# Two layers of a 16-expert MoE block: gate and up with the tokens stationary in layer 0, expert outputs added into SBUF in layer 1

## The reference, cut to what matters

```
aff = softmax(x @ w_router)               # (tokens, 16)
for segment in (latent: C = 64, context: C = 32):     # layer 1: latent only
    idx, g = the C tokens of the segment with the largest aff, for each expert
    xe = x[idx]                                        # (16, C, 1024)
    h  = silu(xe @ w_e_gate) * (xe @ w_e_up)           # (16, C, 1408)
    ye = (h @ w_e_down) * g
    out.at[idx].add(ye)                                # sum over the experts
```

## Time and profile before

| | us |
|---|---|
| median of 3 runs | 3777.25 (3774.8 to 3778.98) |
| the profiled execution: its own time | 3779.97 |
| its span | 3778.2 |
| PE busy | 3457.1 (92%) |
| DVE, ACT, POOL busy | 1099.1, 711.7, 130.8 |
| HBM read and written | 712.57 MB, 25.21 MB |

### The profile page before, as it was taken

The page is one execution under the profiler, slowest core; times in us unless marked ns, Lnnn a source line. Parts: engine busy times, 40 slices in busy tenths (PEclk is TensorE's granted clock), DMA queues, the critical chain, the costliest instruction groups (busy, mean ns, idle before and its releaser), DMA issues.

```text
span 3778.2 us, 66347 instructions
## 1 busy us (share of the span) xinstructions
PE 3457.1 (92%) x27998; PEld 2409.6 (64%) x27998; DVE 1099.1 (29%) x2456; ACT 711.7 (19%) x1362; POOL 130.8 (3%) x188
## 2 busy tenths in 40 slices
PE   7899999999999999999999999998999998888887
PEld 4556757768875677777777666656677564444443
DVE  1443314325533311111111443315264231111112
ACT  2312212012223100000000422220132210101101
POOL 0000100000000000000000000000000000000000
PEclk9999999899999999999999999898999999999999
DMA  5601011010022999999999302020201259999998
GB/s 219 233 32 47 23 56 34 28 51 29 29 112 116 360 346 359 362 371 364 356 371 351 121 1 75 23 78 12 78 29 51 111 228 406 412 411 413 411 412 329
DMA packets 102941, 741.32 MB, mean 196 GB/s; under 512 B 8224, under 2 KB 14496, under 8 KB 60720
## 3 DMA queue, kind: packets, MB, share of 16 engines
q1 hardware_dynamic: 90512, 692.67, 46.5%
q0 software_dynamic: 12192, 45.14, 4.1%
HBM read 712.57 MB, written 25.21 MB: 195 GB/s over the span
## 4 chain that ended last, share of the span: by engine, by line
PE 69%; DMA 21%; DVE 5%; ACT 2%; issue 2%; SPq 0%; DVEq 0%; POOL 0%; ACTq 0%; POOLq 0%
PE psum L633 14%; PE psum L1167 8%; PE psum L535 7%; DMA ring<-in_w_e_down 7%; PE psum L1197 6%; PE psum L528 5%; DMA ring<-in_w_e_gate 5%; DMA ring<-in_w_e_up 4%; PE psum L1023 4%; PE psum L635 3%; PE psum L1158 3%; PE psum L755 2%; DMA work<-in_w_e_gate 2%; PE psum L1203 2%; PE psum L773 2%
## 5 line engine op out<-in xcount | busy, mean ns | idle before, releaser
L633 PE MATMUL psum<-HT,ring 128*128 128x256 f32 x2560 | 621.0, 398 | 19.7 <-DVEq L1918 8.6
L633 PEld LDWEIGHTS psum<-HT,ring 128*128 128x128 f32 x2560 | 504.2, 200 | 119.9 <-issue 28.9
L1167 PE MATMUL psum<-work,ring 128*64 128x96 f32 x11264 | 488.3, 248 | 43.0 <-issue 30.5
L1167 PEld LDWEIGHTS psum<-work,ring 128*64 128x64 f32 x11264 | 474.3, 138 | 59.0 <-issue 46.4
L1158 PE MATMUL psum<-ring,work 128*64 128x256 f32 x1024 | 253.3, 406 | 66.8 <-DMA ring<-in_w_e_gate 52.0
L1338 ACT ACTIVATE work<-psum,small 128x768 f32<-128x768 f32 (+3 forms) x208 | 146.1, 702 | 716.5 <-PE psum L1203 321.0
L535 PE MATMUL psum<-ring,HT 128*128 128x512 f32 (+1 forms) x768 | 276.0, 521 | 0.0
L1158 PEld LDWEIGHTS psum<-ring,work 128*64 128x64 f32 x1024 | 144.3, 146 | 163.5 <-DMA ring<-in_w_e_gate 62.6
L1159 PE MATMUL psum<-ring,work 128*64 128x256 f32 (+1 forms) x1024 | 244.2, 384 | 0.0
L1197 PE MATMUL psum<-ring,work 128*64 128x512 f32 x960 | 222.0, 602 | 9.3 <-DMA ring<-in_w_e_down 9.3
L1341 ACT ACTIVATE work<-psum 128x256 f32<-128x256 f32 (+8 forms) x227 | 107.4, 473 | 652.9 <-PE psum L535 237.8
(11 more groups left out here) (207 smaller groups left out, 3920.4 us busy)
## 6 DMA issues: line engine op xcount, KB each, us to landing
ring<-in_w_e_gate SPq DMA_DIRECT2D x64, 2048.0 KB, 13.0
ring<-in_w_e_up SPq DMA_DIRECT2D x48, 2048.0 KB
ring<-in_w_e_down SPq DMA_DIRECT2D x48, 2048.0 KB
ring<-in_w_ada SPq DMA_DIRECT2D x24, 2048.0 KB, 9.5
ring<-in_w_e_up SPq DMA_DIRECT2D x32, 1536.0 KB, 10.3
ring<-in_w_gate SPq DMA_DIRECT2D x16, 2048.0 KB, 8.8
HT<-in_w_e_up SPq DMA_DIRECT2D x16, 2048.0 KB, 24.8
ring<-in_w_e_gate SPq DMA_DIRECT2D x16, 1536.0 KB
```

What stands on the lines that cost most here:

```text
L633: pe.matmul(b[:, 0:256], w[:, k, d4 * P:(d4 + 1) * P], HT[:, k, off:off + 256], start=(k == 0), stop=(k == KD - 1))
L1167: ins = pe.matmul(b[lo:lo + 64, f * cap:(f + 1) * cap], w[:, k, c0:c0 + 64], e_xs[:, k, 0:cap], start=(k == 0), stop=(k == KD - 1))
```

## The change: what it does, and the diff

Layer 0: `gate_up` keeps the tokens as in layer 1. The 64 latent tokens are stationary in two column groups with up to 256 weight columns streamed through each, and after the eight steps of these the 32 context tokens are stationary in four (or three) column groups with 128 weight columns through each; they write columns 256 to 383 of the same bank. The gated values are now turned by `turn_hidden`, three transposes each time, and copied by ACT (`turned`) into `hid96`. DVE's and ACT's gating handles three shapes for the last 384 columns. PE waits for `idx_next` before `gate_up(2)` instead of after it.

Layer 1: the scatter, the zeroing DMA of `f_rows`, the reads back and the waits on `put` are gone. The sum stays in SBUF (`facc`), zeroed by POOL. The selection of an expert's tokens is written twice side by side (`e_sel2`), turned by four transposes (`rows_of_selection`) after the next expert's first piece, and kept by ACT (`sel_rows`). Both halves of down go to one bank, and ACT alone scales them into `e_ys2`. In the following expert PE multiplies the kept matrix with `e_ys2` for each of the four tiles of 128 tokens, one after each of its first four pieces (`put_back`: two products of 64 rows, in different row groups, 512 columns each, to banks 7 and 5), and DVE adds each into `facc`. At the end all four tiles are summed in PSUM.

```diff
-                            for k in range(KD if two else 0):
+                            for k in range(KD):
                                 b = banks[(0, 2, 0)[g] + u]
                                 pe.matmul(b[0:64, 0:256], e_xs[:, k, 0:64], w[:, k, 0:256], start=(k == 0), stop=(k == KD - 1))
                                 ins = pe.matmul(b[64:128, 0:n - 256], e_xs[:, k, 0:64], w[:, k, 256:n],
                                                 start=(k == 0), stop=(k == KD - 1))
-                            for f in range(0 if two else n // P):
-                                b = banks[(0, 2, 0)[g] + u]
-                                for k in range(KD):
-                                    for half in range(2):
-                                        lo, c0 = 64 * half, f * P + 64 * half
-                                        ins = pe.matmul(b[lo:lo + 64, f * cap:(f + 1) * cap], w[:, k, c0:c0 + 64], e_xs[:, k, 0:cap],
-                                                        start=(k == 0), stop=(k == KD - 1))
+                            for k in range(0 if two else KD):
+                                for q in range(n // P):
+                                    ins = pe.matmul(b[32 * q:32 * q + CAP_C, 256:384], e_xs[:, k, CAP_L:CAPS], w[:, k, q * P:q * P + P],
+                                                    start=False, stop=(k == KD - 1), skip_group_check=True)
...
+                        for j in range(2 if two else 3):
+                            rows = 32 * min(4, NF - 4 * g) if j == 2 else P if 4 * g + 2 + j < NF else 64
+                            c0 = g * (512 if two else 384) + j * P
+                            ins = pe.transpose(b[:, at:at + rows], e_hid[0:rows, c0:c0 + P], ident[0:rows, 0:rows])
...
+                    def put_back(x):
+                        if x:
+                            pe.wait_ge(sems["f_free"], c.nth("f_free"))
+                        for half in range(2):
+                            lo = 64 * half
+                            ins = pe.matmul(banks[PUT[half]], sel_rows[lo:lo + CAP_L, x * P:(x + 1) * P], e_ys2[lo:lo + CAP_L, :],
+                                            start=True, stop=True)
+                        ins.then_inc(sems["f_prod"], 1)
+
+                    def rows_of_selection():
+                        pe.wait_ge(sems["ys_a"], c.nth("ys_a"))
+                        for x in range(NT - CT):
+                            ins = pe.transpose(banks[6][:, x * P:(x + 1) * P], e_sel2[:, x, :, :].rearrange("p i j -> p (i j)"), ident)
+                        ins.then_inc(sems["sel_rows"], 1)
...
+                    if two:
+                        gate_up(0, (first_piece_done, lambda: put_back(1)))
+                        if not last:
+                            choose()
...
+                        gate_up(1, (lambda: put_back(2), lambda: put_back(3)))
+                        if not last:
+                            pe.wait_ge(sems["idx_next"], c.nth("idx_next"))
+                        turn_hidden(0)
+                        gate_up(2)
+                        pe.wait_ge(sems["f_free"], c.nth("f_free"))
+                        turn_hidden(1)
...
+                        pe.wait_ge(sems["sel_kept"], c.nth("sel_kept"))
+                        down(0)
...
                     gate_up(1)
...
+                    else:
+                        pe.wait_ge(sems["idx_next"], c.nth("idx_next"))
+                    turn_hidden(0)
                     gate_up(2)
...
+                    pe.wait_ge(sems["hid_f"], c.nth("hid_f"))
+                    turn_hidden(1)
...
                     down(0)
+                    pe.wait_ge(sems["hid_f"], c.nth("hid_f"))
+                    turn_hidden(2)
                     down(1)
+                    pe.wait_ge(sems["hid_f"], c.nth("hid_f"))
                     down(2)
...
+                if two:                                   # PE, behind the last expert
+                    others(3, (1,))
+                    pe.wait_ge(sems["ys_a"], c.nth("ys_a"))
+                    last_one(0)
+                    last_one(1)
+                    others(2)
+                    last_one(2)
+                    others(3, (0,))
+                    last_one(3)
+                    return
...
+                    if last and cap == 64:                # ACT, before it waits for down
+                        do(s_rt[:, 0:1], s_ms[:, 0:1], AF.Sqrt)
...
+                def put_back(x):                          # DVE
+                    dve.wait_ge(sems["f_prod"], c.nth("f_prod"))
+                    for half in range(2):
+                        f = facc[:, CT + x, half * 512:half * 512 + 512]
+                        tt(f, f, banks[PUT[half]], ALU.add)
+                    dve.sem_inc(sems["f_free"], 1)
...
+                    if cap == 64:                         # DVE, one expert
+                        put_back(0)
+                        hidden(0)
+                        put_back(1)
+                        dve.wait_ge(sems["ys_a"], c.nth("ys_a"))
+                        now_chosen()
+                        if not last:
+                            next_chosen()
+                        put_back(2)
+                        hidden(1)
+                        put_back(3)
+                        hidden(2)
```

More of the change, by code:

```diff
@@ L1110, in choose @@
                     pe.wait_ge(sems["sel"], c.nth("sel"))
-                    for t in range(CT, NT):
+                    for t in range(CT, NT) if two else ():
+                        for half in range(2):
+                            lo = 64 * half
+                            ins = pe.matmul(banks[4][lo:lo + CAP_L, 0:2], e_sel2[:, t - CT, half, :], e_ta[:, t, :],
+                                            start=(t == CT), stop=(t == NT - 1))
+                    for t in () if two else range(CT, NT):
                         for lo in (0, 64):
@@ L1147, in weight, with gate_up @@
                         return slot(n0 + SHARED[i][0], n, k)
-                    def gate_up(g):
+                    def gate_up(g, then=(None, None)):
                         for u in range(2):
@@ new lines, in expert @@
+                    pe.wait_ge(sems["xs"], c.nth("xs"))
+                    if two:
[3 more added lines that the diff above has]
+                        else:
+                            back = rings["a"][-1][1]
+                            ring("a", (4,))
+                            gate_rows(early_diag[L])
+                            ring("a", back)
+                        gate_up(1, (lambda: put_back(2), lambda: put_back(3)))
[6 more added lines that the diff above has]
+                        if not last:
+                            turn_rows()
+                        else:
+                            others(1)
+                        pe.wait_ge(sems["sel_kept"], c.nth("sel_kept"))
+                        down(0)
+                        turn_hidden(2)
+                        if last:
+                            others(0)
+                        down(1)
+                        down(2)
+                        return
@@ L1240, in expert @@
                     down(0)
-                    if two:
-                        turn_hidden(2)
+                    pe.wait_ge(sems["hid_f"], c.nth("hid_f"))
+                    turn_hidden(2)
                     down(1)
+                    pe.wait_ge(sems["hid_f"], c.nth("hid_f"))
                     down(2)
@@ L1250, in turn_selection, with others @@
                     ins.then_inc(sems["sel_t"], 1)
-                def others(x):
-                    pe.wait_ge(sems[f"f_back{FIRST[x]}"], c.nth(f"f_back{FIRST[x]}", 16))
-                    pe.nop(nofuse=True)
-                    for half in range(2):
+                def others(x, halves=(0, 1)):
+                    if not two:
+                        pe.wait_ge(sems[f"f_back{FIRST[x]}"], c.nth(f"f_back{FIRST[x]}", 16))
+                        pe.nop(nofuse=True)
+                    for half in halves:
                         cols = slice(half * 512, half * 512 + 512)
-                        pe.matmul(summed[x][:, cols], ident, facc[:, FIRST[x], cols], start=True, stop=False)
+                        pe.matmul(summed[L][x][:, cols], ident, facc[:, CT + x, cols], start=True, stop=False)
                 def last_one(x):
@@ L2421, in moe @@
                 t0, nq = QT[0], len(QT)
-                S(dve.memset(e_sel, 0.0))
+                if L == 0:
+                    S(dve.memset(e_sel, 0.0))
                 ts(e_ta[:, :, 0], cc("tokens"), -float(first_row[L]), ALU.add)
@@ L2485, in expert @@
                         ahead_of_seam()
+                    if cap == 64:
+                        put_back(0)
+                        hidden(0)
+                        put_back(1)
+                        dve.wait_ge(sems["ys_a"], c.nth("ys_a"))
+                        now_chosen()
+                        if not last:
+                            next_chosen()
```

(18 more changed lines are left out.)

140 lines of the change are left out of this document (83 added, 57 removed).

## The result

Over 20 runs of each, the changed kernel takes 3787.68 us (median; 3777.35 to 3795.86) and the kernel before 3777.96 (3767.09 to 3785.42): a ratio of 1.0024, 95% interval 1.0017 to 1.0032. It is slower, by 9.7 us where I forecast 27. The profiled executions take 3795.42 us (span 3793.7) and 3779.97 (3778.2). Divided at the first matmul of a layer's experts and the last of its down, the difference of 15.4 us is +22.4 in layer 0's experts, -9.0 in layer 1's and the tail behind them, and about +2 in stages that the diff leaves alone.

What follows compares the result with a forecast made beforehand. The prediction took layer 0 to be bound by PE and layer 1 by transfers; +42 us in layer 0 and -15 in layer 1 made +27 on the profiled 3780.0, 3804 by the median, range 3772 to 3842.

Steps and rivals of the forecast that it cites:

- rival (3): Layer 0's pauses all go and layer 1's scatters were dear: +27 and -20 us, 3784 in all; chance 0.12.
- Layer 0, blocks and turns: Layer 0's experts: gate and up blocks cost +3.5 us an expert, three added turns +1.7 us.
- Layer 0, pauses: Layer 0's experts: PE's pauses, taken as instructions coming late, shrink to 0.7 us an expert, a gain of 2.6 us.
- Rival (2): Layer 0's gate_up is bound by transfers, longer blocks only fill pauses: layer 0 at 0, 3759 in all; chance 0.13.
- Rival (1): Layer 0's pauses stay as long as they are: +83 us there, +68 in all, 3845; chance 0.13.
- Layer 1, scatters and the loop: Layer 1's experts: removed scatters give -16 us; put_backs are hidden except in expert 0, +4 us.
- Rivals (4) and (5): Layer 1: scatter time isn't given back, PE refilling late, or put_backs hold up the loop at DVE: 3819; chance 0.15.
- Layer 1, the end: Layer 1's end: shorter last products, fewer identity products before them and an earlier table load, about -3 us.

Runs made afterwards that it cites:

- e4: The changed kernel with layer 0's latent products of gate and up cut into halves of 128 streamed columns, so more instructions for the same columns: 3813.40 us.
- e2: The changed kernel with layer 0 as before, so only layer 1's half of the change: 3766.68 us, 0.9977 of the kernel before.
- e3: The kernel before with layer 1's scatters left out and nothing in their place: 3760.37 us, 0.9964 of the kernel before.
- e6: e2 with layer 0's first 15 experts in a hardware loop on PE: 3883.71 us, 1.0278 of the kernel before.
- e8: e7 with two more of layer 0's groups considered, only the first group of 512 columns on tokens, the others on kept weights: 3868.14 us.
- e7: e5 with layer 0's first 15 experts in a hardware loop on PE: 3734.76 us, 0.9882 of the kernel before.
- e10: The changed kernel with layer 0's experts in a hardware loop on PE and nothing else: 3785.49 us, 1.0027 of the kernel before.
- e5: The changed kernel with layer 0's group of 384 columns keeping the weights as before, without its turn: 3745.88 us, 0.9917 of the kernel before.
- e9: e7 with one sum of the last expert's second layer moved behind down: 3732.23 us, 0.9887 of the kernel before.

## Why the prediction was wrong

The direction, the bound of each stage and the blocks were right, and the time lies in the range, though just below the 3788 to 3824 that the forecast gave itself, and nearer to rival (3)'s 3784. The sum was 27 and the result 9.7, since two terms failed. They failed in opposite directions: I had layer 0 some 20 us too dear and layer 1's gain 6 us too large. That they cancel in part is luck.

**Layer 0, blocks and turns: right.** Six pieces of 5.49 us instead of 5.46. The turns take 0.48 before gate_up(2), 0.39 before turn_rows and 0.69 us between down's blocks, 1.5 in all for 1.7. Together they are +5.1 us an expert, for the 5.2 forecast.

**Layer 0, pauses: this step failed.** I put them at 2.9 to 3.5 us an expert (3.3 in the sum) and let 0.7 remain, so that 2.6 went. With the blocks at +5.1 and the step at +1.53, 3.6 went. The error is the size before. An expert before is 46.0 us of blocks: 29.3 for gate and up, 0.8 each for choose and turn_rows, 15.05 for down. So its step of 50.25 held 4.3 us of pauses, while the earlier trace rows show 3.2 as idle time. More than half of the other 1.1 us is in how a pause is counted. The list takes it from the modelled end of the last product, 0.25 us after its start, where the next one ordinarily starts 0.04 us after it. So each pause in a piece is listed 0.2 us short: by the starts of the products, the 38 waits listed inside the pieces of 14 experts are 38.9 us, where the list has 31.1. That is 0.6 us an expert; the remaining 0.5 was not followed up. I should have built the sum of blocks and taken the pauses as what it leaves of the step; I read them off a list. What remains was sized about right: the changed kernel's blocks are 51.07 us (its expert 0), so 0.7 us of its step are waits, though all of those listed are for weights and none is on issue. "Gate and up now use 96 pairs in 5.46 us" was the right mechanism, and closer to a threshold than to the proportion I gave it, although 80 instruction packets are still fetched: at 96 products a piece no issue pause is left, at 128 (e4) 1.3 us of them by the list.

The steps make 16 of the 20 us that layer 0 missed by. The last expert makes the other 3: it is no longer than before (54.2 us for 54.8), where I had +2.6. Part of this is chance. The same code as before took 51.7 us there in e2 and 50.1 in e3, with shorter waits for down's weights than the 2.3 us of this execution. Together layer 0 is +22.4 instead of +42. Rival (3) had the pauses all going, and its +27 for layer 0 was nearer; even that kept too small a size for them (3.5 us), and so was above the 22.4. Rival (2), layer 0 bound by its transfers and so no longer than before, falls with the +22.4 at a DMA share of 0.94.

That the pauses are instructions coming late was argued in the prediction and is now shown: they come with the number of instructions at the same work (e4), each ends 1.2 to 1.6 us after an instruction packet (before, e4), and with a loop that fetches its instructions anew they grow (e6, e8). Where no packet is fetched (e7, e10), 0.4 and 0.6 us are left in 14 experts; but e5 and the changed kernel had only 1.9 and none to lose, and e4's kernel in a loop that fits was not tried. Rival (1) falls with the changed kernel itself, which has no issue pause though its queues are nearly as full (a DMA share of 0.94 for 0.96).

The Trainium skill, page "TensorEngine Tiling (Array Packing)", section "Instruction Overhead", gives each matmul about 60 cycles of its own, by which e4's 157 added products would cost about 3.9 us an expert (an estimate from the page, at the full clock); its blocks show 0.2, so by this rule the trace doesn't agree where products in two column groups follow each other.

**Layer 1, scatters and the loop: right.** Experts 1 to 14 went from 606.6 to 591.4 us, -15.2 where 14 scatters of 1.05 us are -14.7 (by the steps of e3 a scatter is 1.16), and the second queue's share from 4.9 to 2.1% (I wrote 2.5). Rivals (4) and (5) fall: the step is e3's. Expert 0 is +5.3 for +4, of which expert 1 gives 0.6 back. The put_backs pair, as forecast. PE's timeline at the first, then DVE's two additions for it:

```profile
3731.26 0.66 PE L1234 MATMUL psum<-const,X 128*128 128x128 f32 x4
3731.85 1.13 PE L1225 MATMUL psum<-work,selT 64*128 64x512 f32 x4
```

```profile
3733.03 1.41 DVE L1921 TENSOR_TENSOR YT<-YT,psum 128x512 f32<-128x512 f32 x2 [13.32 <-PE psum L1225]
```

**Layer 1, the end: this step failed too.** With the last scatter I had -4 us for the last expert and the tail; it was +1: -2.4 in the tail, near the -3 forecast, and +3.3 in the last expert, whose neighbours I had not looked at. Before, PE waited there for down's weights, and the identity products stood behind down:

```profile
3742.48 0.44 PE L1179 MATMUL psum<-const,X 128*128 128x128 f32 x2
3743.87 3.65 PE L1197 MATMUL psum<-ring,work 128*64 128x512 f32 x16 [0.95 <-DMA ring<-in_w_e_down]
...
3748.82 1.94 PE L1197 MATMUL psum<-HT,work 128*64 128x512 f32 x8 [0.83 <-DMA YT<-in_w_e_down]
...
3755.21 1.98 PE L1258 MATMUL psum<-YT,const 128*128 128x512 f32 x4
```

After, two pairs of them and the four put_backs stand ahead of down's end, no wait for down's weights is left, and PE is what is late:

```profile
3758.88 0.44 PE L1190 MATMUL psum<-const,X 128*128 128x128 f32 x2
3759.16 1.88 PE L1316 MATMUL psum<-YT,const 128*128 128x512 f32 x4
3760.97 3.65 PE L1209 MATMUL psum<-ring,work 128*64 128x512 f32 x16
...
3765.02 1.98 PE L1316 MATMUL psum<-YT,const 128*128 128x512 f32 x4
...
3773.09 1.12 PE L1316 MATMUL psum<-YT,const 128*128 128x512 f32 x2
```

"The last rows' products take 1.0 instead of 2.0 us and only one half of an identity product stands before them" was right of what lies behind down, and silent on where the rest of the identity products went: each is 1.9 us. The layer's total is -15.2 + 5.3 + 0.9 = -9.0, where I had -15.

The profiled pair differs by 15.4 us and the medians by 9.7; some 2 us of the pair's difference lie in stages without an edit, and the rest is within what single executions scatter (18 us between the fastest and slowest of before). The stage sums stand for the pair alone.

## What to carry to other kernels

Where an engine pauses in the middle of a straight run of small instructions, add up its blocks and take the rest of the step as pauses; then ask for fewer instructions or a hardware loop whose body fits, not for shorter streams. A new form is worth its price only in the pieces where it costs less than the pauses that it takes away. Here that is 0.2 us and a turn in a piece of 512 columns, and 1.5 us in one of 384: with one group left as it was and a loop, the same change takes the kernel from 0.24% slower to 1.18% faster (3734.76 us; 3732.23 with e9's edit). Work moved "to an idle place" at the end of a layer needs that place read too: the last pass has other neighbours than the loop.

## What the runs showed of the hardware that was not expected

- A hardware loop on PE runs without instruction transfers with a body of 759 products and their weight loads, and not with 815. Past that it is worse than no loop: 125 packets in 14 experts (e6) instead of 96 (e2), stalls of up to 5.9 us at the head of the body, and then 4.4 us at half the clock. Where between the two the limit lies, and whether it counts other instructions too, wasn't measured; and the bodies that are fetched anew are also those with two or three groups on the kept weights, so size and form were not varied apart.
- e7's loop took 1 us an expert off e5, though e5's issue pauses were only 1.9 us in 14 experts; what fell is the wait for weights, from 17.4 us to 6.2 in 14 experts. The 83 instruction packets of e5 are 1.36 MB, under 4 us at its 368 GB/s, so most of that fall stays open.
- A pause of PE for instructions ends 1.2 to 1.6 us after a packet of the instruction queue has landed, in 38 of 38 cases in the kernel before and 28 of 28 in e4. Most packets have no pause behind them (58 of 96 before, all 80 after).
- Three column groups of 32 columns streaming 128 each take as long (1.88 us for 48 products) as four (64 products).
